# A two-block transformer kernel: the router's share expansion spread over four expert units, and the first projection's products reordered around the last attention chunk

## The reference

```python
proj = rmsnorm(h) @ w_in                      # pool_v, q, k, v, r, g_lr
y_pool = pool_mixer(pool_v)                   # window means, 4 groups of 128 channels
o = gated_linear_attention(q, k, v, g_lr)     # 5 chunks of up to 64 tokens, 4 heads of 128
o = o * rsqrt(mean(o*o, over a head) + eps) * gla_norm_w * silu(r)
h = h + concat(y_pool, o) @ w_out
x = rmsnorm(h)
combine = router(x)                           # 1 of 4 groups, then 2 of its 4 experts; 256 x 16 weights
for e in range(16):                           # every expert is computed for every token
    y += combine[:, e:e+1] * ((silu(x @ w_gate[e]) * (x @ w_up[e])) @ w_down[e])
```

## Time and profile before

| | us |
|---|---|
| median of three runs | 2266.02 |
| lowest to highest | 2263.27 to 2266.15 |
| the profiled execution, whole | 2264.65 |
| its span | 2262.9 |
| mean granted TensorE clock in it | 0.985 of full |

### The profile page before, as it was taken

One profiled execution on the slowest core, in us unless ns is written; L12 is line 12 of the kernel. 1 busy time (PEld: TensorE's weight loads), 2 busy tenths in 40 slices (PEclk: granted clock), 3 DMA queues, 4 the chain that ended last, 5 costly groups with the idle time before them and its releaser, 6 DMA issues.

```text
span 2262.9 us, 31830 instructions
## 1 busy us (share of the span) xinstructions
PE 2189.6 (97%) x13281; PEld 1906.8 (84%) x13281; DVE 1369.8 (61%) x1770; ACT 764.9 (34%) x1075; POOL 519.6 (23%) x243
## 2 busy tenths in 40 slices
PE   7988999999999999989999999999999999899998
PEld 7878999988888888857988888898888888679998
DVE  6557876577776237795677773246564226665444
ACT  4334444432222222274422222232222213354443
POOL 0013632112222110153122221112222010243431
PEclk9888999999999999999999999999999999999999
DMA  5236886656664336400365663345564335204664
GB/s 162 93 95 172 218 220 191 178 166 177 171 184 127 101 89 190 112 20 29 102 192 171 178 174 90 90 118 171 182 187 136 91 102 145 89 13 134 183 170 147
DMA packets 474005, 314.68 MB, mean 139 GB/s; under 512 B 27503, under 2 KB 435958, under 8 KB 473862
## 3 DMA queue, kind: packets, MB, share of 16 engines
q1 hardware_dynamic: 434304, 237.02, 37.5%
q10 hardware_dynamic: 39558, 75.64, 10.9%
HBM read 311.56 MB, written 1.05 MB: 138 GB/s over the span
## 4 chain that ended last, share of the span: by engine, by line
PE 86%; DVE 8%; ACT 3%; DMA 1%; issue 1%; SPq 0%; POOL 0%; DVEq 0%; ACTq 0%
PE ps L1805 26%; PE ps L1807 25%; PE ps L1806 25%; DVE w_lo L1018 2%; PE ps L1987 2%; ACT w_hi L597 2%; PE ps L1798 2%; PE ps L2417 1%; PE ps L2379 1%; DVE st L1644 1%; DVE u_lo L1111 1%; DMA raw<-in_w_in 1%; DVE tmp_a L1103 1%; PE ps L2385 1%; DVE ada_acc L1039 1%
## 5 line engine op out<-in xcount | busy, mean ns | idle before, releaser
L1805 PE MATMUL ps<-u_hi,w_hi 128*128 128x256 f32 (+2 forms) x2624 | 888.1, 338 | 22.1 <-DVE w_lo L1018 10.8
L1807 PE MATMUL ps<-u_hi,w_lo 128*128 128x256 f32 (+2 forms) x2624 | 876.3, 334 | 0.0
L1806 PE MATMUL ps<-u_lo,w_hi 128*128 128x256 f32 (+2 forms) x2624 | 876.1, 334 | 0.0
L1018 DVE TENSOR_TENSOR w_lo<-raw,w_hi 128x2048 fp32r<-128x2048 f32 (+1 forms) x238 | 503.4, 2115 | 340.1 <-ACT w_hi L597 340.0
L597 ACT CAST w_hi<-raw 128x2048 fp32r<-128x2048 f32 (+1 forms) x238 | 418.1, 1757 | 467.8 <-PE ps L1807 430.7
L1805 PEld LDWEIGHTS ps<-u_hi,w_hi 128*128 128x128 f32 x2624 | 501.4, 191 | 75.1 <-DVE w_lo L1018 16.5
L1807 PEld LDWEIGHTS ps<-u_hi,w_lo 128*128 128x128 f32 x2624 | 501.2, 191 | 48.9
L1806 PEld LDWEIGHTS ps<-u_lo,w_hi 128*128 128x128 f32 x2624 | 501.7, 191 | 46.9
L1726 POOL TENSOR_TENSOR hf_lo<-tmp_b,hf_hi 128x512 fp32r<-128x512 f32 (+1 forms) x88 | 240.4, 2732 | 713.4 <-ACT hf_hi L740 713.4
L1039 DVE SCALAR_TENSOR_TENSOR ada_acc<-ada_w,sc_c,ada_acc 128x512 f32<-128x512 f32 x448 | 347.4, 831 | 6.7 <-DMA ada_w<-in_w_ada 1.2
L737 ACT ACTIVATE tmp_a<-ps 128x512 f32<-128x512 f32 (+1 forms) x120 | 60.2, 501 | 710.0 <-PE ps L1807 545.6
(11 more groups left out here) (310 smaller groups left out, 1882.5 us busy)
## 6 DMA issues: line engine op xcount, KB each, us to landing
ada_w<-in_w_ada ACTq DMA_DIRECT2D x144, 512.0 KB, 4.0
raw<-in_w_ffn_gate SPq DMA_DIRECT2D x88, 512.0 KB, 4.0
raw<-in_w_ffn_up SPq DMA_DIRECT2D x88, 512.0 KB, 5.3
raw<-in_w_in SPq DMA_DIRECT2D x52, 512.0 KB, 5.0
raw<-in_w_ffn_down SPq DMA_DIRECT2D x64, 384.0 KB, 3.6
raw<-in_w_ffn_down SPq DMA_DIRECT2D x64, 320.0 KB, 4.2
raw<-in_w_expert_gate SPq DMA_DIRECT2D x32, 512.0 KB, 4.3
raw<-in_w_expert_up SPq DMA_DIRECT2D x32, 512.0 KB, 5.6
```

The source lines that it names most:

```text
L1018: tt(w_lo[:, slot, 0:elems], raw[:, slot, 0:elems], w_hi[:, slot, 0:elems].bitcast(F32), ALU.subtract).then_inc(lo_done.sem, 1)
L1805: mm(acc, w1, m_hi, start=(first and i == 0), stop=False)
L1806: mm(acc, w1, m_lo, start=False, stop=False)
L1807: ins = mm(acc, w2, m_hi, start=False, stop=(last and i == n - 1))
```

## The change

It has four parts.

1. **Deferred shares.** TensorE turns the logits inside expert unit 0 (after its first 12 matmuls) and the shares inside unit 1 (after 36). It expands four experts' shares inside each of units 2 to 5, after their first 12 matmuls. ScalarE and VectorE start the units' work at once, and copy the shares four at a time behind units 1 to 4. Units 0 and 1 are multiplied with their share afterwards, in `tmp_b`. The router's tiles are moved behind `comb` in memory (`router_pad`).
2. **Modulation quarters of `moe_a`** go to units 3, 4, 6, 8, 10, 11, 13, 15, 17, 18, 20, 22, 24, 25, 27 and 29. The sums move to units 11, 18 and 25.
3. **Projection order.** On VectorE, `pooled_low(2, 4)` goes between `chunk_out(3)` and `chunk_scores(4)`, and `chunk_out(4)` goes behind the split of `out1`'s unit 1. TensorE does one part of the pooled half ahead of `out_step(4)` and two behind it; the heads' means, the fourth part and the spread follow in that order.
4. **Heads' norm by tokens.** The means are taken with tokens on the partitions, eight one-column products into 128 x 8. Root and reciprocal work on 128 x 8, and eight 128 x 128 products against the identity spread the factors.

```diff
--- before.py
+++ after.py
@@ -439,6 +440,9 @@
             if ada is None:
                 return [], None
             first, chunks, every, each, start = ADA[ada]
+            if ada == "moe_a":
+                done = {11: 0, 18: 1, 25: 2}
+                return [(q // 4, q % 4) for q in range(16) if 3 + 7 * q // 4 == n], done[n] if n in done else None
             n -= start
             if n < 0:
                 return [], None
...
@@ -831,7 +835,7 @@
             nc.scalar.activation(proj1[:, 0:4, N_META:T1], oT[:, :, N_META:T1], ACT.Square).then_inc(ev["o_sq"], 1)
             nc.scalar.activation(root_one[:, :], one, ACT.Sqrt)
             act.wait_ge(ev["o_ms"], 1)
-            nc.scalar.activation(rstd[0:4, 0:SEQ], ps[0:4, 4, 0:SEQ], ACT.Sqrt, bias=eps[0:4, :]).then_inc(ev["o_root"], 1)
+            nc.scalar.activation(head_inv[:, :], ps[:, 4, 0:8], ACT.Sqrt, bias=eps).then_inc(ev["o_root"], 1)
             for j in range(2):
                 act.wait_ge(ev["gla_out"], j + 1)
                 nc.scalar.copy(u_hi[:, 4 + 2 * j:6 + 2 * j, N_META:T1], oT[:, 2 * j:2 * j + 2, N_META:T1]).then_inc(ev["gla_high"], 1)
...
@@ -845,10 +849,34 @@
             nc.scalar.activation(r4b[:, :, :], r4a[:, :, :], ACT.Exp).then_inc(ev["g_exp"], 1)
             act.wait_ge(ev["e_shift"], 1)
             nc.scalar.activation(prob[:, :, :], r4c[:, :, :], ACT.Exp).then_inc(ev["e_exp"], 1)
-            for e in range(0, N_EXPERTS, 2):
-                act.wait_ge(ev["share_sum"], e + 1)
-                nc.scalar.copy(comb[:, e, :], ps[:, 4 + e % 4, 0:SEQ]).then_inc(ev["share_out"], 1)
-            ffn_up(st_moe_a, moe_sig, SEQ, MOE_F, hm_hi, "moe_a")
+            def even_shares(i):
+                for e in range(4 * i, 4 * i + 4, 2):
+                    act.wait_ge(ev["share_sum"], e + 1)
+                    nc.scalar.copy(comb[:, e, :], ps[:, 4 + e % 4, 0:SEQ]).then_inc(ev["share_out"], 1)
+            def expert_high(n):
+                if n < 2:
+                    act.wait_ge(moe_sig["comb"].sem, moe_sig["comb"].at(n + 1))
+                else:
+                    act.wait_ge(acc_free.sem, st_moe_a["g0"] + n + 1)
+                nc.scalar.copy(hm_hi[:, n, :], tmp_b[:, n % 2, 0:SEQ]).then_inc(moe_sig["hi"].sem, 1)
+            for n in range(MOE_F):
+                for c, quarter in ada_at("moe_a", n)[0]:
+                    ada_load(0, c, quarter)
+                g = st_moe_a["g0"] + n
+                act.wait_ge(unit_done.sem, st_moe_a["u0"] + n + 1)
+                need(act, acc_free, g - 1)
+                nc.scalar.activation(tmp_a[:, n % 2, 0:SEQ], ps[:, 2 * (g % 2), 0:SEQ], ACT.Silu).then_inc(moe_sig["silu"].sem, 1)
+                next_hi(st_moe_a, 0, n)
+                if 1 <= n <= 4:
+                    even_shares(n - 1)
+                if n == 1:
+                    expert_high(0)
+                if n >= 1:
+                    expert_high(n)
             n0, e1 = norm_of["l0a"], norm_of["end1"]
...
@@ -1395,8 +1420,6 @@
                     split_lo(1, 1, UNIT)
                     dve.wait_ge(ev["low_sum"], 1)
                     nc.vector.tensor_copy(glr[:, :], ps[:, 4, 0:T1]).then_inc(ev["low_out"], 1)
-                if i == 7:
-                    chunk_out(4)
                 split_lo(i + 2, i % 2, UNIT)
                 if i == 0:
                     context(0)
...
@@ -1423,17 +1446,18 @@
                     chunk_scores(3)
                     chunk_state(2)
                     chunk_out(3)
+                    pooled_low(2, 4)
                     chunk_scores(4)
                     chunk_state(3)
-            pooled_low(2, 4)
+            chunk_out(4)
             dve.wait_ge(ev["silu_r"], 1)
             gw = VEC["gla_norm"][0]
             dve.wait_ge(ev["o_out"], 4)
             stt(out=proj1[:, 12:16, N_META:T1], in0=oT[:, :, N_META:T1], scalar=vec[:, gw:gw + 1], in1=proj1[:, 12:16, N_META:T1],
                 op0=ALU.mult, op1=ALU.mult).then_inc(ev["gated"], 1)
             dve.wait_ge(ev["o_root"], 1)
-            nc.vector.reciprocal(rstd[0:4, 0:SEQ], rstd[0:4, 0:SEQ]).then_inc(ev["o_inv"], 1)
+            nc.vector.reciprocal(head_inv[:, :], head_inv[:, :]).then_inc(ev["o_inv"], 1)
             dve.wait_ge(ev["gated"], 1)
             dve.wait_ge(ev["o_sq"], 1)
             for j in range(2):
...
@@ -1508,17 +1532,52 @@
                          oh_g[:, t, :].rearrange("p (g o) -> p g o", o=1).to_broadcast([P, 4, 4]),
                          r4a[:, t, :].rearrange("p (o k) -> p o k", o=1).to_broadcast([P, 4, 4]), ALU.mult)
             ins.then_inc(ev["shares"], 1)
-            dve.wait_ge(ev["shares_turned"], 1)
-            link(nc.vector.tensor_copy(combT[:, :], ps[0:16, 7, 0:SEQ]))
-            nc.vector.tensor_copy(pick[:, :], ident[0:16, 0:16])
-            link(nc.vector.tensor_copy(comb_hi[:, :], combT[:, :]))
-            tt(comb_lo[:, :], combT[:, :], comb_hi[:, :].bitcast(F32), ALU.subtract).then_inc(ev["shares_out"], 1)
-            for e in range(1, N_EXPERTS, 2):
-                dve.wait_ge(ev["share_sum"], e + 1)
-                nc.vector.tensor_copy(comb[:, e, :], ps[:, 4 + e % 4, 0:SEQ]).then_inc(ev["share_out_odd"], 1)
-            dve.wait_ge(ev["share_out"], N_EXPERTS // 2)
-            dve.wait_ge(ev["share_out_odd"], N_EXPERTS // 2)
+            def shares_split():
+                dve.wait_ge(ev["shares_turned"], 1)
+                link(nc.vector.tensor_copy(combT[:, :], ps[0:16, 7, 0:SEQ]))
+                nc.vector.tensor_copy(pick[:, :], ident[0:16, 0:16])
+                link(nc.vector.tensor_copy(comb_hi[:, :], combT[:, :]))
+                tt(comb_lo[:, :], combT[:, :], comb_hi[:, :].bitcast(F32), ALU.subtract).then_inc(ev["shares_out"], 1)
+            def odd_shares(i):
+                for e in range(4 * i + 1, 4 * i + 4, 2):
+                    dve.wait_ge(ev["share_sum"], e + 1)
+                    nc.vector.tensor_copy(comb[:, e, :], ps[:, 4 + e % 4, 0:SEQ]).then_inc(ev["share_out_odd"], 1)
+            def share_ready(e):
+                dve.wait_ge(ev["share_out_odd" if e % 2 else "share_out"], e // 2 + 1)
+            def experts_up():
+                sig, slot = moe_sig, lambda n: tmp_b[:, n % 2, 0:SEQ]
+                for n in range(MOE_F):
+                    g = st_moe_a["g0"] + n
+                    work, complete = ada_at("moe_a", n)
+                    if complete is not None:
+                        ada_out(complete)
+                    dve.wait_ge(sig["silu"].sem, sig["silu"].at(n + 1))
+                    if n >= 2:
+                        share_ready(n // 2)
+                        tt(tmp_a[:, n % 2, 0:SEQ], tmp_a[:, n % 2, 0:SEQ], comb[:, n // 2, :], ALU.mult).then_inc(sig["comb"].sem, 1)
+                        dve.wait_ge(sig["comb"].sem, sig["comb"].at(n + 1))
+                    need(dve, sig["lo"], n - 1)
+                    tt(slot(n), tmp_a[:, n % 2, 0:SEQ], ps[:, 2 * (g % 2) + 1, 0:SEQ], ALU.mult).then_inc(acc_free.sem, 1)
+                    if 1 <= n <= 4:
+                        odd_shares(n - 1)
+                    next_lo(st_moe_a, 0, n)
+                    if n == 0:
+                        shares_split()
+                    if n == 1:
+                        share_ready(0)
+                        for m in range(2):
+                            dve.wait_ge(acc_free.sem, acc_free.at(st_moe_a["g0"] + m + 1))
+                            tt(slot(m), slot(m), comb[:, 0, :], ALU.mult).then_inc(sig["comb"].sem, 1)
+                    for c, quarter in work:
+                        ada_quarter(c, quarter)
             def modulation(l, nw, m):
                 t0 = 72 * l + 8 * m
...
@@ -1848,15 +1907,17 @@
                              start=True, stop=True)
                 ins.then_inc(n["spread"].sem, 1)
-            def two_tiles(u, g, cols, T, ready=None, c0=0, inside=None):
+            def two_tiles(u, g, cols, T, ready=None, c0=0, inside=None, router=None):
                 slot = u % 2
                 if ready is None:
-                    for t, k0, k1 in ((0, 0, 4), (0, 4, KD), (1, 0, KD)):
+                    for t, k0, k1 in ((0, 0, 4), (0, 4, KD), (1, 0, 4), (1, 4, KD)) if router else ((0, 0, 4), (0, 4, KD), (1, 0, KD)):
                         ins = products(ps[:, 2 * g + t, 0:T], slot, [cols(t, k) for k in range(k0, k1)],
                                        rows_of(u_hi, u_lo, k0, k1 - k0, T, c0), T, k0 == 0, k1 == KD)
-                        if k1 == 4 and inside is not None:
+                        if t == 0 and k1 == 4 and inside is not None:
                             ada_sums(inside)
+                        if router and router[0:2] == (t, k1):
+                            router[2]()
                 else:
                     for k in range(KD):
                         pe.wait_ge(ready.sem, ready.at(k + 1))
...
@@ -2207,25 +2266,29 @@
```

(50 more changed lines are left out.)

10 lines of the change are left out of this document (4 added, 6 removed).

## The result

The changed kernel took 2250.47 us in the median of five runs (2247.16 to 2253.97), beside 2264.61 us for the kernel before. The ratio is 0.9934, with a 95% interval of 0.9921 to 0.9947: 14.1 us faster by the medians. A gain of 16.7 us had been forecast, to 2247.95 us for the profiled execution and 2249.3 for the median, and the range was 2245.5 to 2256. By the medians the gain is 14.1 us, 2.6 less than forecast; 1.4 of these lie in the kernel before, whose median is 2264.61 us over five runs where it was 2266.02 over three.

What follows compares the result with a forecast made beforehand. TensorE's own matmul stream, busy 97% of the span, was taken as the bound. Projection 5.6 + router and experts 11.4 - quarters 0.3 = 16.7 us off 2264.65 gave 2247.95, median 2249.3; range 2245.5 to 2256.

Steps and rivals of the forecast that it cites:

- The middle case for the clock: Projection: clock low before out_step(4), full through it, low again for 16 of 24 pooled products; 5.6 us gained.
- the wait of 1.43: Projection, behind the spread: a new TensorE wait of 1.5 us for the attention half's low rows.
- the clock doesn't come back in front of `out_step(4)`: Rival, projection: clock stays low through out_step(4); projection gives 3.1 us, in all 14.2, to 2251.8 us; chance 0.18.
- My 131.7: Projection: third unit's start in us if the clock stays low until the 24 pooled products are through; gain 3.1 us.
- The rule of the page: Clock gate set by recent busy time: gapless TensorE would keep 2.4 GHz through out_step(4); doubted for narrow products.
- 11.4 - 0.3: Gain of 11.4 us from the last router product through the experts, less 0.3 us for modulation quarters in pairs.
- The slacks that I had counted up to unit 2: Experts: shares' weights 1.8 us early (166.36 for 168.2), unit 2's weights at 169.1 for 170.0, split at 170.3 for 171.5.
- The 0.7 us that I had put in for changes and clock: Experts: cost of switches between share groups and a few products before the clock is back.
- The pairs of quarters: Modulation quarters at units 10 and 11, 17 and 18, 24 and 25: costed at 0.3 us, between 0 and 2.5.
- one of the signs that I had named for being wrong: Experts: TensorE waiting for w_lo in units 2 to 6 or behind the pairs of modulation quarters.
- that rival: Weights late in the experts, 1 to 2 us at several of 4 pairs, some 4 to 5 us: 2254; chance 0.14.
- Slower, or nothing moved: Two rivals: VectorE behind in units 2 to 5, 2267 to 2270, chance 0.04; waits come back, 2262 to 2267, chance 0.05.

Runs made afterwards that it cites:

- again: The changed kernel run a second time with no edit: 2249.74 us, ratio 0.9934 to the kernel before.
- again_b: The changed kernel run a third time with no edit: 2248.17 us.
- e_proj: The kernel before with only the projection's part (pooled_low, order of products, norm by tokens) as changed: 2262.65 us, ratio 0.9988.
- e_evenada: The changed kernel with the expert stage's modulation quarters back in their former places, one in every even unit: 2249.73 us.
- e_rownorm: The changed kernel with the heads' norm in its former form (four rows of 256 tokens), in the new order: 2250.98 us, ratio 0.9934.
- e_split4: The changed kernel with the fourth pooled part cut in two, six products on either side of the spread: 2248.17 us, ratio 0.9919.
- split4_b: The changed kernel with the fourth pooled part cut in two around the spread, measured a second time: 2248.02 us.
- e_router: The kernel before with only the deferred shares and the modulation quarters as changed, projection as before: 2254.62 us, ratio 0.9956.

## Why the prediction was right, step by step

**The projection.** 5.6 us were forecast from the end of the last scores to the third unit, and 6.6 came in the first trace. The middle case for the clock was the one that this execution and `again` ran: low in front of `out_step(4)`, full through it (2.8 us for 2.9), low behind it. Then the steps: means 1.7 for 1.8, the wait of 1.43 for 1.5, the weights' 1.55 for 1.6. The mis-sized term is the spread, put at 2.7 us by the row of two such products, where eight products (sixteen records) took 1.95. The rest of the 1.0 us is `out_step(4)`, which ended at 109.7 and not at 110.1; the low stretch behind it ended with some 9 products left, where I had 8.

The rival "the clock doesn't come back in front of `out_step(4)`" is not wrong but the other half of the truth. `again_b`, `e_proj` and `e_evenada` ran it, and all three have a distance of 53.7 us. My 131.7 makes 54.0, counted from the first scores product of before (77.7). Eight traces have this order up to the heads' means (the three of the changed kernel, `e_proj`, `e_evenada`, `e_rownorm`, `e_split4`, `split4_b`): five ran the middle case and three the rival, more than its chance of 0.18. That the first trace ran the middle case was partly luck. So the projection's gain isn't one number: it is 6.3 or 3.5 us by the distances, against a before that itself moves (57.2 us, and 58.6 in `e_router`). That fits a median gain of 14.1 us beside a profiled execution, the fastest of its five, at 17.5. That the place of the clock's fall explains all of the 7 us between runs was not shown. Only traced executions have it, and the three of the changed kernel also differ by 1.1 us ahead of the first scores product and by 1.3 us behind the experts.

**The rule of the page.** In no trace did a TensorE without gaps keep the clock through the chunks, unless wide products stood between the narrow ones. By the Trainium skill, page "TensorE: Matmul & The Clock Gate", section "Part 1: The HAM clock gate", activity releases the throttle, and how busy the engine has been sets it. If busy is what the profile calls busy, the row of the changed kernel with 3.70 of 3.70 us busy and the fall behind it speak against the rule for narrow products, and the woven kernel shows that it is their lying in one piece that matters.

**Router and experts.** 11.4 - 0.3 = 11.1 us were forecast, and 12.0 came, alike in three traces of the changed kernel to 0.5 us. Of the 12.0 us, 8.5 are waits that are gone (5.9, 1.3 and 1.3). The rest lies where the clock stood at 0.50, at the start of unit 2 in before; in the changed kernel it stands at 1.00 from 151.0 to 170.5. The slacks that I had counted up to unit 2 held: shares at 159.8 for 161.6, weights of unit 2 at 162.3 for 163.3, the table load in front of the wait. The logits cost a wait of 0.27 us that I had at nothing. The 0.7 us that I had put in for changes and clock were too much. The pairs of quarters, costed at 0.3 with a slack of 0.2 to 0.3 us, cost nothing that a median shows (`e_evenada`). The wait of 0.48 us behind the first pair in `again_b` is one of the signs that I had named for being wrong. It came in one of three traces, and at a tenth of the 4 to 5 us of that rival.

**Slower, or nothing moved.** Neither: VectorE's longest units (3 and 4, with copies and a quarter) made TensorE wait not once in the three traces of the changed kernel.

## What to carry to other kernels

When an engine's in-order program puts a long side task (here 16 copies, eight on each of two engines) ahead of the work that feeds TensorE, cut the task and lay the pieces behind that work; a producer that multiplies a weight in afterwards buys the time. When a reorder fills TensorE's idle time, ask what is then left to lay behind the next wait: here the filler was moved away from the 1.4 us that it had covered. And price such an order at both levels of the clock, since the same products ran at either in different executions.

## What the hardware showed that I had not expected

- Weaving narrow fp32 products between wide ones kept the full clock from 80 to 117.6 us, but cost up to 0.3 us for each round, more than the clock gave back: the projection took 52.7 us with 3.4 us at 1.2 GHz, against 50.8 us with 10.2 us at 1.2 GHz.
- The same stretch of the projection took 50.8, 50.8 and 53.7 us in three executions. In the third the clock stood at 1.2 GHz for 17.1 us instead of 10.2. The third unit's start (128.2, 127.1 and 130.1 us) hides this, since the stretch itself began up to 1.1 us apart.
- A four-row reciprocal over 256 columns took 1.74 us and the one over 128 x 8 took 0.20 us; the products around them cost nearly the same in both forms.
